# The attention mask: an identity matmul on PE, or an add by DVE on the scores in PSUM

## What is computed

```python
def one_block(args):
    q_blk, k_blk, v_blk, blk_idx = args
    s = jnp.einsum('bqkgd,bckd->bkgqc', q_blk, k_blk).astype(jnp.float32) * ATTN_SCALE
    valid = in_band & ((blk_idx > 0) | (kc >= WINDOW))
    s = jnp.where(valid, s, -jnp.inf)
    m = jnp.maximum(jnp.max(s, axis=-1, keepdims=True), sink)
    p = jnp.exp(s - m)
    w = p / (jnp.sum(p, axis=-1, keepdims=True) + jnp.exp(sink - m))
    return jnp.einsum('bkgqc,bckd->bqkgd', w.astype(v_blk.dtype), v_blk)
```

## Time and profile before

| | |
|---|---|
| median of 3 executions | 2467.03 us (2464.87 to 2467.62) |
| the profiled execution | 2467.14 us, of which the span from first to last instruction is 2465.3 us |
| mean granted PE clock | 0.997 |
| attention units | about 1522 to 1681 us of the span |
| busy in the span | PE 98%, DVE 66%, ACT 46%, POOL 3% |

### The profile page before, as it was taken

How to read it: one execution, slowest core, us unless ns; L and a number is a source line. 1 busy time by engine, 2 the same in 40 slices (tenths; PEclk the granted TensorE clock), 3 DMA queues, 4 the chain that set the end, 5 groups by cost and what they waited for, 6 DMA issues and landing times.

```text
span 2465.3 us, 33685 instructions
## 1 busy us (share of the span) xinstructions
PE 2424.5 (98%) x12336; PEld 2051.9 (83%) x12336; DVE 1616.7 (66%) x2163; ACT 1141.4 (46%) x1583; POOL 68.8 (3%) x83
## 2 busy tenths in 40 slices
PE   7999999999999999999999999999999999999998
PEld 6888888888888888888888888888888888888886
DVE  6888888886568556556556576655875655654655
ACT  4545544554345445445444454453643443443542
POOL 0100100000000000000000000000000000000000
PEclk9999999999999999999999999999999999999999
DMA  7555656545557666566566545225665655655653
GB/s 217 166 167 163 170 162 170 170 137 211 207 171 223 223 193 188 192 188 189 196 189 187 195 151 201 103 95 196 179 222 192 187 192 190 187 188 188 194 190 111
DMA packets 486485, 446.17 MB, mean 181 GB/s; under 512 B 13616, under 2 KB 359904, under 8 KB 485072
## 3 DMA queue, kind: packets, MB, share of 16 engines
q1 hardware_dynamic: 484608, 433.52, 56.3%
q0 software_dynamic: 1744, 10.81, 1.2%
HBM read 442.18 MB, written 2.10 MB: 180 GB/s over the span
## 4 chain that ended last, share of the span: by engine, by line
PE 92%; DVE 4%; ACT 2%; DMA 1%; issue 1%; POOL 0%; DVEq 0%; SPq 0%; ACTq 0%
PE ps L442 25%; PE ps L460 15%; PE ps L462 15%; PE ps L461 15%; PE ps L444 13%; DVE wlo L1265 2%; PE ps L513 2%; PE ps L595 1%; ACT whi L837 1%; PE ps L494 1%; PE ps L492 1%; PE ps L493 1%; PE ps L750 1%; PE ps L730 1%; DMA raw<-in_mlp_w 0%
## 5 line engine op out<-in xcount | busy, mean ns | idle before, releaser
L1265 DVE TENSOR_TENSOR wlo<-raw,whi 128x1024 fp32r<-128x1024 f32 x818 | 998.1, 1225 | 564.2 <-ACT whi L837 556.1
L837 ACT ACTIVATE whi<-raw 128x1024 fp32r<-128x1024 f32 x818 | 861.3, 1057 | 765.3 <-PE ps L462 521.9
L442 PE MATMUL ps<-actA,whi 128*128 128x512 f32 x2704 | 963.0, 400 | 6.2 <-DVE wlo L1265 4.9
L444 PE MATMUL ps<-actA,wlo 128*128 128x256 f32 x2704 | 760.0, 281 | 0.0
L442 PEld LDWEIGHTS ps<-actA,whi 128*128 128x128 f32 x2704 | 509.6, 188 | 132.2 <-issue 7.2
L444 PEld LDWEIGHTS ps<-actA,wlo 128*128 128x128 f32 x2704 | 512.5, 190 | 2.7 <-issue 1.7
L460 PE MATMUL ps<-whi,actB 128*128 128x512 f32 x1056 | 412.6, 391 | 0.0
L462 PE MATMUL ps<-whi,actB 128*128 128x512 f32 x1056 | 411.0, 389 | 0.0
L461 PE MATMUL ps<-wlo,actB 128*128 128x512 f32 x1056 | 410.9, 389 | 0.0
L462 PEld LDWEIGHTS ps<-whi,actB 128*128 128x128 f32 x1056 | 198.2, 188 | 41.6
L460 PEld LDWEIGHTS ps<-whi,actB 128*128 128x128 f32 x1056 | 198.2, 188 | 40.9
(11 more groups left out here) (222 smaller groups left out, 1808.7 us busy)
## 6 DMA issues: line engine op xcount, KB each, us to landing
raw<-in_mlp_w SPq DMA_DIRECT2D x512, 512.0 KB, 3.9
raw<-in_a_w_in SPq DMA_DIRECT2D x162, 512.0 KB, 4.0
raw<-in_a_w_out SPq DMA_DIRECT2D x64, 512.0 KB, 4.0
raw<-in_b_w_q SPq DMA_DIRECT2D x32, 512.0 KB, 4.5
raw<-in_b_w_o SPq DMA_DIRECT2D x32, 512.0 KB, 3.6
raw<-in_kv_w SPq DMA_DIRECT2D x16, 512.0 KB, 3.5
gb<-in_ln_g POOLq DMA_DIRECT2D x4, 1024.0 KB, 7.5
gb<-in_ln_b POOLq DMA_DIRECT2D x4, 1024.0 KB, 10.0
```

The lines of the kernel that those rows point to most:

```text
L442: e.matmul(ps[:, b, :].rearrange("p (a n) -> p a n", a=2), whi[:, s, w], act[:, kt, :, :], start=(kt == 0), stop=False)
L444: last = e.matmul(ps[:, b, T:2 * T], wlo[:, s, w], act[:, kt, 0, :], start=False, stop=(kt == KT - 1))
L837: e.activation(whi[:, s, :], raw[:, r, :], ACT.Copy).then_inc(w_hi_done, C.up(w_hi_done))
L1265: e.tensor_tensor(wlo[:, s, :], raw[:, r, :], whi[:, s, :].bitcast(F32), ALU.subtract).then_inc(w_split, C.up(w_split))
```

## The change

The mask no longer enters through PE. `scores` issues only the matmuls of queries with keys, each with `start=True, stop=True`, in the same banks. In `maxima`, ahead of the reduction, DVE adds the mask in place on the scores in PSUM, 128x512 for c = 0 and 128x1024 for c = 1, and the reduction waits for it. The mask is kept in float32, the float32r identity is gone, and with it one ACT copy.

The first unit of blocks 1 to 3 (units 4, 8 and 12) transposes its probabilities in bank 7 in place of bank 6, so `p_transposes` of these units does not wait for `output(u-1)` to free bank 6. Their `values` waits until ACT has emptied bank 7, and the output transposes of the unit before, which use bank 7, come behind them.

```diff
+P_BANK = [7 if b and (c, j) == (0, 0) else 6 for b, c, j in UNITS]
...
-                if c == 0:
-                    fill(4)
-                    e.matmul(ps[:, 4, :].rearrange("p (h n) -> p h n", h=4), ident_r[:, :],
-                             amask_r[:, 1, :].unsqueeze(1).broadcast_to([P, 4, P]), start=True, stop=False)
-                    for i in range(4):
-                        last = e.matmul(ps[:, 4, i * P:(i + 1) * P], qT[:, i, 0:P], kz[:, kv, 0:P],
-                                        start=False, stop=(i == 3))
...
+                w = (1 + c) * P
+                for bank in range(4, 5 + c):
+                    fill(bank)
                     for i in range(4):
+                        if bank == 4 + i * w // BLK:
+                            k = i * w % BLK
+                            last = e.matmul(ps[:, bank, k:k + w], qT[:, i, c * P:(c + 1) * P], kz[:, kv, 0:w],
+                                            start=True, stop=True)
+                    last.then_inc(full[bank], C.up(full[bank]))
+
+            def p_transposes(c, bank):
                 e.wait_ge(exps_ready, C.next(exps_ready))
                 if c == 0:
-                    transposes(6, [pb[:, i, 0:P] for i in range(4)])
+                    transposes(bank, [pb[:, i, 0:P] for i in range(4)])
...
-            def values(b, c, j):
+            def values(b, c, j, bank):
                 kv = 2 * b + j
-                if c:
+                if c or bank == 7:
                     emptied(7)
...
-                e.activation(ident_r[:, :], ident[:, :], ACT.Copy)
...
-            def pT_out():
-                e.wait_ge(full[6], C.next(full[6]))
-                e.activation(pT[:, 0:4, :], tiles(6), ACT.Copy).then_inc(free[6], C.up(free[6]))
+            def pT_out(b):
+                e.wait_ge(full[b], C.next(full[b]))
+                e.activation(pT[:, 0:4, :], tiles(b), ACT.Copy).then_inc(free[b], C.up(free[b]))
...
                 src = ps[:, 4:5 + c, :].rearrange("p a (h n) -> p (a h) n", n=w)
+                mask = amask[:, 1 - c:2, :].rearrange("p a n -> p (a n)")
+                e.tensor_tensor(src, src, mask.unsqueeze(1).broadcast_to([P, 4, w]), ALU.add).then_inc(
+                    dve_step, C.up(dve_step))
+                e.wait_ge(dve_step, C.now(dve_step))
                 e.tensor_reduce(mx, src, AX.X, ALU.max).then_inc(dve_step, C.up(dve_step))
```

More of the change, by code:

```diff
@@ L207, in build @@
     ident = place("ident", [P, P])
-    ident_r = place("ident_r", [P, P], F32R)
     tri = place("tri", [P, P])
-    amask_r = place("amask_r", [P, 2, P], F32R)
+    amask = place("amask", [P, 2, P])
     csx = place("csx", [P, NH, 2, P], F32R)
@@ L789, in attention @@
                 for u, (b, c, j) in enumerate(UNITS):
-                    p_transposes(c)
+                    p_transposes(c, P_BANK[u])
                     if u + 1 < len(UNITS):
@@ L795, in attention @@
                         o_transposes()
-                    values(b, c, j)
+                    values(b, c, j, P_BANK[u])
                     turn = (c, j) == (1, 0) and b < QB - 1
@@ L875, in constants_out @@
                 e.wait_ge(consts_in, C.next(consts_in))
-                e.activation(ident_r[:, :], ident[:, :], ACT.Copy)
                 e.activation(tri[:, :], kst[:, K_TRI:K_TRI + P], ACT.Copy)
-                e.activation(amask_r[:, :, :].rearrange("p a n -> p (a n)"), kst[:, K_AMASK:K_AMASK + 2 * P], ACT.Copy)
+                e.activation(amask[:, :, :].rearrange("p a n -> p (a n)"), kst[:, K_AMASK:K_AMASK + 2 * P], ACT.Copy)
                 e.activation(selg[:, :], kst[:, K_SEL:K_SEL + 4 * GH], ACT.Copy).then_inc(
@@ L1211, in attention @@
                 for u, (b, c, j) in enumerate(UNITS):
-                    pT_out()
+                    pT_out(P_BANK[u])
                     if c:
@@ L1861, in sums, with output @@
                 e.reciprocal(rinv, den).then_inc(dve_step, C.up(dve_step))
-            def output(b, c, j):
-                e.wait_ge(full[6], C.next(full[6], 2))
+            def output(b, c, j, p_bank):
+                e.wait_ge(full[6], C.next(full[6], 2 if p_bank == 6 else 1))
                 e.wait_ge(dve_step, C.now(dve_step))
@@ L1894, in attention @@
                         pT_out()
+                    elif P_BANK[u] == 7:
+                        C.n[full[7]] += 1
+                        C.n[free[7]] += 1
                     if u + 1 < len(UNITS):
@@ L1902, in attention @@
                         o_lo(u - 1)
-                    output(b, c, j)
+                    output(b, c, j, P_BANK[u])
                     if (c, j) == (1, 0) and b < QB - 1:
@@ L2036, in _ @@
             norm_rstd()
-FULLS = {0: {4: 26, 5: 27, 6: 35, 7: 27}, 2: {4: 46, 5: 39, 6: 77, 7: 53}}
+FULLS = {0: {4: 26, 5: 27, 6: 35, 7: 27}, 2: {4: 46, 5: 39, 6: 74, 7: 56}}
 TOTAL = 2 + NG * GROUP_CHUNKS + 2 * SLAB_CHUNKS + 8 * 2 * SLAB_CHUNKS + 16 + 32 + 32
```

## The result

| | median us | lowest to highest, executions | ratio to before (95%) |
|---|---|---|---|
| before | 2466.34 | 2462.25 to 2467.62, 7 | 1 |
| changed | 2473.70 | 2472.37 to 2475.24, 7 | 1.0026 (1.0017 to 1.0036) |
| changed, a second time | 2477.84 | 2476.19 to 2480.12, 4 | 1.0045 (1.0030 to 1.0061) |

The change makes the kernel slower, by 0.26% in the first comparison; forecast were 2474 us, and a chance of 0.56 for slower by over 0.2%. The ratios are those on record and not the quotients of the two medians, which would be 1.0030 and 1.0046. One of the twelve executions of the last version under the experiments took 8638 us, and one of the 29 of the kernel before beside it 2677 us; they are left out of the ratios.

A forecast was written before the change was run, and what follows sets the result against it. DVE was taken as the bound from unit 2's scores to unit 3's exponent bias, though PE is 98% busy overall. 2467.1 + 2.8 for shifted waits + 4.2 for two clock falls gave 2474 us, range 2467 to 2480.

The forecast's parts named there:

- What PE saves: Attention scores: 24 mask matmuls of 0.23 us leave PE, or 5.5 us.
- The price of the add: DVE, ahead of each maximum: scores-to-exponentials way grows by 0.73 us (128x512) and 1.27 us (128x1024), wait included.
- Bank 7: Transposes of units 4, 8 and 12 no longer wait for `otok`: 0.57 us wait plus 0.19 us refilling gained, three times.
- the sum: Whole attention stage, all shifts of PE added with its clock unchanged: +2.8 us, giving 2469.9 us.
- The new wait: PE ahead of the transposes of units 2, 6 and 10, for `otok` to free bank 6: 0.47 us.
- the one ahead of the query transposes: PE in units 2, 6 and 10, waiting for `o_lo`: grows from 0.31 to 2.65 us.
- unit 15's: PE's wait in unit 14, ahead of unit 15: 0.70 + 1.27 = 2.0 us, which may add another clock fall.
- A block: Shift of PE over one block against before: +0.86 us, three blocks and the start making +2.12.
- The two figures that were to bound it: Idle time of PE before its clock falls: between 2.1 and 3.3 us, with the new 2.65 us waits between.
- two falls at the turns: PE's clock falls in two of the three 2.65 us waits, 2.1 us lost each: +4.2 us.
- the adds are harmless or cheap: Two rivals: DVE absorbs the adds, 2460.9 us, chance 0.07; adds of 0.7 us or less, about 2466, chance 0.07.
- the clock holds in all three waits: Rival at the three 2.65 us query-transpose waits: no clock fall, 2469.9 us, chance 0.31.

The follow-up runs named there:

- the last version under the experiments: Changed kernel with DVE adding the mask only for 128-key units except unit 13, plus both query transposes in mid second filler chunk: 2461.73 us, ratio 0.9983.
- the filled wait: Changed kernel with 11 unused 512-column matmuls in the wait ahead of the query transposes in units 2, 6 and 10: 2469.94 us, ratio 1.0016.
- the mask part alone: Changed kernel without its bank part: all units transpose probabilities in bank 6, the mask stays on DVE: 2478.33 us, ratio 1.0037.
- turn halfway: Changed kernel with both transposes of the next queries in the middle of the turn unit's second filler chunk: 2466.70 us, ratio 1.0002.
- bank part alone: Changed kernel with the mask added by PE again as before, units 4, 8 and 12 using bank 7: 2464.19 us, ratio 0.9985.
- add only where it is covered: Changed kernel with DVE adding the mask only for units of 128 keys except unit 13, PE for the others, bank 7 kept: 2462.80 us, ratio 0.9986.

## Why the prediction was right

**What PE saves.** 24 matmuls less, as said. Without the add the stage is 6.4 us shorter. The matmuls and the bank are worth 7.8 us, 7.6 of them within the stage length; 0.46 us is waited out at each of the three turns, since PE then merely comes earlier to the wait.

**The price of the add.** Taken from rows of the same sizes on other operands, 0.69 and 1.23 us, and 0.04 us for its wait: both as measured. The way over two adds is 2.51 us longer in the trace, which is 1.26 us each. The Trainium skill, VectorE: DVE Perf Modes, "The DRAIN you can't avoid", says that the semaphore costs nothing extra; by that the prediction estimated 1.15 us for an add, and this trace does not agree.

**Bank 7.** Three times 0.76 us, covered with 0.5 us to spare by the sum: alone it gave 2.2 us, and no wait took its place. Only with the add issued twice did a unit wait for its exponentials.

**Where it lands.** The new wait was put at 0.47 us and is 0.45 to 0.47; the one ahead of the query transposes at 2.65 and is 2.61 to 2.64; unit 15's at 2.0 and is 1.98. Two terms were a little too large. At unit 12 0.33 us was taken, and the wait grew by 0.23 (1.06 to 1.29). A block was summed to +0.86 us; with the clock at 1.00 it takes 37.69 us from turn to turn, before 36.92 (1562.90 to 1599.82), which is +0.77. So the sum would be some 2.4 us instead of 2.8. The kernel with the filled wait took 2469.94 us, the 2469.9 of the sum, but that is in part chance: one fall is left in it. From the transposes of unit 15 to the end of the stage it takes 6.6 us, where the second profile of the changed kernel, without a fall there, takes 5.3; that makes the fall 1.3 us of its stage of 156.1.

**The clock.** That it would fall at waits of 2.65 us was right, and that PE's idleness does it, as the filled wait shows. The two figures that were to bound it, 2.1 and 3.3 us after the last matmul, are no bounds: in these runs the falls of the stage begin from 1.2 us after the start of PE's wait (the second profile, first turn) to 4.0 us after it (the add issued twice, third turn), in the wait or behind it. And the kernel before has near 544 us a wait of 2.15 us at which the clock stayed at 1.00, a row that the prediction overlooked. The size was right in the first comparison partly by luck. Taken were two falls at the turns of 2.1 us each, +4.2. The first profile has one at a turn and one behind unit 14's wait, 2.9 us together; the second has three at the turns, 160.1 - 155.1 = 5.0 us. In the stage lengths a low stretch of 3.4 us comes to some 1.5 us and one of 6.8 us to 2.0 to 2.5. So the term is a spread, here of 3 to 5 us and in the kernel with the mask part alone of 9, more than one number. Nor is the whole difference from this stage: in the two profiled executions the span grew by 7.9 us, 4.7 ahead of the stage, 5.9 in it and 2.7 less behind it, while the forecast put all of it into the stage. The medians of the two comparisons, 2473.70 and 2477.84, lie 4 us apart with the same waits, those of the kernel before, 2466.34 and 2466.53, hardly at all. That falls of the clock make all of these 4 us is argued from two profiles and not shown; it stays open.

**The rivals.** That the adds are harmless or cheap is out by their durations and by the run without them. DVE had no slack between the scores of unit 2 and the bias of unit 3; the 31% of that stretch in which it idles lie ahead of the one and behind the other. That the clock holds in all three waits is out by both profiles of the changed kernel.

## What to carry to other kernels

Before work is moved from the busiest engine to one that idles a third of the time, follow the receiving engine's queue in order of time: where it runs without a gap from a result of the first engine to something that the first will wait for, the added work comes back in full at that wait. Here, three times over, two adds of 1.23 us came back for four matmuls of 0.23. A long wait that is left is best given matmuls that are due anyway (2466.70 us here, with unused ones 2469.94); and a change can be split by units: seven of the 128x512 adds cost nothing here, the eighth, in unit 13, goes ahead of a wait that grew by 0.23 us, and the 128x1024 adds are the dear ones.

## What the runs showed of the hardware that was not expected

- At a wait of 1.97 or 1.98 us, or up to 1.3 us behind it, PE's clock fell in four executions (changed, mask alone, turn halfway, filled wait) and not in a fifth, the second profile of the changed kernel. At waits of 2.61 to 2.64 us it fell in seven of nine cases: one of three in the changed kernel, three of three in its second profile and with the mask alone. With the add issued twice it fell at all six waits of 2.02 us and more. At waits of up to 1.3 us it never fell in this stage, nor at two of 1.74 us. The Trainium skill, TensorE: Matmul & The Clock Gate, "Why this matters for your kernels", puts its limit for such gaps above the waits of 1.97 to 2.64 us; the measured rows decide.
- Matmuls whose results nobody uses made the kernel faster: with 33 more of 512 columns it took 2469.94 us, 1.0016 (1.0007 to 1.0025), where the changed kernel beside it on the same chip took 2477.84, 1.0045 (1.0030 to 1.0061).
- The clock also falls in stages that the change doesn't touch: its mean was 0.91 in 540 to 560 and in 760 to 780 us of the changed kernel's first profile, and 1.00 in both in the one before. Near 544 us all eleven profiles have a wait of PE of 2.15 to 2.18 us; the clock fell behind it in eight and held in three (before, bank part alone, add only where it is covered). So the same wait lowers the clock in one execution and not in another. It may be part of why whole executions differ by microseconds, and it is why the stage length was the finer measure.

The wait near 544 us, here in the kernel before:

```profile
544.83 0.47 PE L460 MATMUL ps<-whi,actA 128*128 128x512 f32 x1 [2.15 <-DVE actA L1277]
```
